# A two-block network with streamed weights: the first products of each FFN and MLP taken chunk by chunk, down products two steps behind

## What is computed

```python
def rms_norm(x, gain):
    y = xf * lax.rsqrt(jnp.mean(xf * xf, axis=-1, keepdims=True) + EPS)
    return (y * gain.astype(jnp.float32)).astype(x.dtype)

def swiglu(h, w13, w2):                       # hidden width 2816
    gate, up = jnp.split(h @ w13, 2, axis=-1)
    return (jax.nn.silu(gate) * up) @ w2

x = x + 0.5 * swiglu(rms_norm(x, ffn1_norm[l]), ffn1_w13[l], ffn1_w2[l])

def sq_relu_mlp(u, w1, w2):                   # hidden width 4096
    a = jnp.maximum(u @ w1, 0.0)
    return (a * a) @ w2

mod = (sc @ w_mod[l] + b_mod[l])[:, None, :]  # 1024 x 6144 for each of two l
mod_c = scc @ w_mod[l] + b_mod[l]             # the same weights for the context
```

## Time and profile before

| | us |
|---|---|
| three runs | 1719.1, 1723.56, 1721.61 |
| median | 1721.61 |
| profiled execution | 1721.9, of which the span 1720.1 |
| PE busy | 1617.6 (94%) |
| DVE busy | 1200.9 (70%) |
| ACT busy | 784.5 (46%) |

### The profile page before, as it was taken

One profiled execution on the slowest core, in us unless ns is written; L12 is line 12 of the kernel. 1 busy time (PEld: TensorE's weight loads), 2 busy tenths in 40 slices (PEclk: granted clock), 3 DMA queues, 4 the chain that ended last, 5 costly groups with the idle time before them and its releaser, 6 DMA issues.

```text
span 1720.1 us, 30317 instructions
## 1 busy us (share of the span) xinstructions
PE 1617.6 (94%) x12454; PEld 1545.4 (90%) x12454; DVE 1200.9 (70%) x1651; ACT 784.5 (46%) x1121; POOL 47.0 (3%) x46
## 2 busy tenths in 40 slices
PE   6999996999999899999789999999789999889999
PEld 6999996899999899999579999996358999879999
DVE  6887788888877677778647877654667656565654
ACT  5434458444445344446544444431445444454442
POOL 1000010100001100001001000000001000010000
PEclk9999998899999899999889999999799999989999
DMA  6766633476665366664124765621124554325450
GB/s 264 269 238 251 227 148 122 163 270 229 245 244 196 123 244 248 234 234 166 50 98 158 270 237 223 250 101 50 70 80 171 181 188 178 122 101 194 172 194 24
DMA packets 43434, 310.83 MB, mean 181 GB/s; under 512 B 4816, under 2 KB 5072, under 8 KB 6096
## 3 DMA queue, kind: packets, MB, share of 16 engines
q1 hardware_dynamic: 41904, 303.33, 47.5%
q0 software_dynamic: 864, 5.21, 0.9%
q10 hardware_dynamic: 576, 1.05, 0.2%
HBM read 308.52 MB, written 1.05 MB: 180 GB/s over the span
## 4 chain that ended last, share of the span: by engine, by line
PE 65%; DVE 11%; ACT 4%; issue 1%; POOL 1%; POOLq 0%; DVEq 0%; ACTq 0%
PE psum L1413 20%; PE psum L1418 19%; PE psum L1419 19%; DVE w_lo L806 4%; DVE buf L815 1%; PE psum L1574 1%; ACT w_hi L416 1%; PE psum L1472 1%; PE psum L1829 1%; DVE u_lo L906 1%; DVE x L885 1%; PE psum L1768 1%; POOL buf L372 1%; PE psum L1562 1%; DVE tiny L1319 0%
## 5 line engine op out<-in xcount | busy, mean ns | idle before, releaser
L1413 PE MATMUL psum<-u_hi,w_hi 128*128 128x256 f32 (+2 forms) x2608 | 761.1, 292 | 38.4 <-DVE u_lo L893 14.3
L1418 PE MATMUL psum<-u_lo,w_hi 128*128 128x256 f32 (+2 forms) x2608 | 750.3, 288 | 0.0
L1419 PE MATMUL psum<-u_hi,w_lo 128*128 128x256 f32 (+2 forms) x2608 | 750.0, 288 | 0.0
L806 DVE TENSOR_TENSOR w_lo<-raw,w_hi 128x1024 fp32r<-128x1024 f32 x480 | 565.3, 1223 | 163.0 <-ACT w_hi L416 162.8
L1413 PEld LDWEIGHTS psum<-u_hi,w_hi 128*128 128x128 f32 x2608 | 508.8, 195 | 48.5 <-issue 16.0
L416 ACT ACTIVATE w_hi<-raw 128x1024 fp32r<-128x1024 f32 x480 | 478.3, 1046 | 129.3 <-PE psum L1413 122.3
L1418 PEld LDWEIGHTS psum<-u_lo,w_hi 128*128 128x128 f32 x2608 | 509.2, 195 | 2.0
L1419 PEld LDWEIGHTS psum<-u_hi,w_lo 128*128 128x128 f32 x2608 | 508.5, 195 | 1.2
L1413 PE MATMUL psum<-hid_hi,w_hi 128*128 128x256 f32 x1220 | 346.4, 284 | 7.0 <-DVE hid_lo L1296 3.7
L1418 PE MATMUL psum<-hid_lo,w_hi 128*128 128x256 f32 x1220 | 345.4, 283 | 0.0
L1419 PE MATMUL psum<-hid_hi,w_lo 128*128 128x256 f32 x1220 | 345.3, 283 | 0.0
(11 more groups left out here) (205 smaller groups left out, 1007.9 us busy)
## 6 DMA issues: line engine op xcount, KB each, us to landing
raw<-stream SPq DMA_DIRECT2D x288, 1024.0 KB, 4.8
buf<-tab POOLq DMA_DIRECT2D x2, 768.0 KB, 4.6
x<-x_in SPq DMA_DIRECT2D x1, 1024.0 KB, 6.9
buf<-ctx_in POOLq DMA_DIRECT2D x1, 1024.0 KB, 5.1
buf<-poolmat POOLq DMA_DIRECT2D x1, 1024.0 KB, 5.1
out<-x ACTq DMA_DIRECT2D x4, 256.0 KB, 2.4
cst<-consts POOLq DMA_DIRECT2D x1, 864.0 KB, 9.0
buf<-late POOLq DMA_DIRECT2D x1, 640.0 KB, 4.3
```

The source lines that it names most:

```text
L806: ve.tensor_tensor(w_lo[:, u], raw[:, u], w_hi[:, u].bitcast(F32), ALU.subtract).then_inc(S.lo_ready, 1)
L1413: ins = te.matmul(dst, w_hi[:, w], hi, start=first, stop=False, skip_group_check=True)
L1418: te.matmul(dst, w_hi[:, w], lo, start=False, stop=False, skip_group_check=True)
L1419: return te.matmul(dst, w_lo[:, w], hi, start=False, stop=last, skip_group_check=True)
```

## The change

`by_chunk` takes several `up` units at once: for each k it waits for the operand, then makes the product of that k for every unit. In ffn1 to ffn3 these are the four units of steps 0 and 1, in ffn0 the two of step 0, in the MLPs the first three (the fourth follows by itself). The norm's product comes after them (in ffn0 after up 1) and goes to bank 0; step 2 of a SwiGLU uses bank 7. In a SwiGLU `down` j now follows up j+2, with four slots of 256 columns for `hid`, and the stream's order follows (`LAG`). `MODS_AT` moves modulation units: two each in steps 3 to 7, one from step 8. After hidden(j) DVE and ACT pump up to the unit before down j, so down j-1, up j+2 and the modulation units of j+2. Ahead of `rms` two more units of the FFN are split (up to its unit 7). The MLPs keep their lag of one. Left out below: the views `ff_hi`, `ff_lo`, `ff_hif`, the same `pump_to` and `early` edits in ffn2 and ffn3, and the bank of the ctx norm on DVE.

```diff
...
-MODS_AT = [0, 0] + [2, 1] * 4 + [1] * (FFS - 10)
+LAG = 2
+MODS_AT = [0, 0, 0, 2, 2, 2, 2, 2, 1, 1] + [1] * (FFS - 10)
...
-    FF_ORDER += [("up", _j)] * 2 + [("mod", _j)] * MODS_AT[_j] + [("down", _j - 1)] * (_j > 0)
-FF_ORDER += [("down", FFS - 1)]
+    FF_ORDER += [("up", _j)] * 2 + [("mod", _j)] * MODS_AT[_j] + [("down", _j - LAG)] * (_j >= LAG)
+FF_ORDER += [("down", FFS - _j) for _j in range(LAG, 0, -1)]
...
-NORM_BANK = {"ffn3": 0}
+NORM_BANK = {n: 0 for n in ("start", "wout", "ctx", "wo", "ffn3", "woe", "pool")}
...
+UP_BANK = [4, 5, 7] + [4 + _j % 2 for _j in range(3, FFS)]
...
-                    sc.activation(hid_hi[:, j % 2, 0:T], h32[:, 0:T], ACT.Copy).then_inc(S.hid_hi_ready, 1)
-
-                pump_to(c0 + ff_at("down", 0) - 1)
+                    sc.activation(ff_hi[:, j % 4, :], h32[:, 0:T], ACT.Copy).then_inc(S.hid_hi_ready, 1)
+
                 for j in range(FFS - 2):
                     hidden(j)
-                    pump_to(c0 + ff_at("down", j + 1) - 1)
+                    pump_to(c0 + ff_at("down", j) - 1)
...
-            pump_to(ff_at("down", 0) - 1)
+            pump_to(7)
...
-            gain_operand("ffn2_0", "wout", early=AT["ffn1"] + 4)
+            gain_operand("ffn2_0", "wout", early=AT["ffn1"] + 8)
...
-                    ve.tensor_tensor(t2.rearrange("p (k t) -> p k t", k=2), bank2(4 + par), over2(rstd[:, :]),
+                    ve.tensor_tensor(t2.rearrange("p (k t) -> p k t", k=2), bank2(UP_BANK[j]), over2(rstd[:, :]),
                                      ALU.mult).then_inc(S.up_scaled, 1)
...
-                    ve.tensor_tensor(hid_lo[:, par, 0:T], h32[:, 0:T], hid_hif[:, par, 0:T], ALU.subtract)\
+                    ve.tensor_tensor(ff_lo[:, j % 4, :], h32[:, 0:T], ff_hif[:, j % 4, :], ALU.subtract)\
                       .then_inc(S.hid_ready, 1)
 
-                pump_to(c0 + ff_at("down", 0) - 1)
                 for j in range(FFS - 2):
                     hidden(j)
-                    pump_to(c0 + ff_at("down", j + 1) - 1)
+                    pump_to(c0 + ff_at("down", j) - 1)
                     if j in MOD_READ:
                         read_modulation(MODG * int(name[3]) + MOD_READ.index(j))
                 hidden(FFS - 2)
+                pump_to(c0 + FFU - 1)
                 read_modulation(MODG * int(name[3]) + MODG - 1)
                 pump_to(c0 + FFU + 3)
                 hidden(FFS - 1)
...
             update_and_operand("wout", "ffn1", "ffn2_0", 1.0)
-            pump_to(AT["ffn1"] + 3)
...
-                te.matmul(psum[:, 7, 0:T], ones, buf[4][:, 0:T], start=True, stop=True).then_inc(S.ms_psum, 1)
-
-            def product(dst, c, at, hi, lo, first, last):
+                if name == "ctx":
+
+                    pe.wait_ge(S.v_out, 1)
+                te.matmul(psum[:, NORM_BANK.get(name, 7), 0:T], ones, buf[4][:, 0:T], start=True, stop=True)\
+                  .then_inc(S.ms_psum, 1)
+
+            def product(dst, c, at, hi, lo, first, last, begins=None):
 
                 w = slice((c % RING) * UNIT + at, (c % RING) * UNIT + at + P)
                 ins = te.matmul(dst, w_hi[:, w], hi, start=first, stop=False, skip_group_check=True)
-                if begun[0] != c:
+                if begun[0] != c if begins is None else begins:
 
                     ins.then_inc(S.unit_used, 1)
...
-            def all_k(c, i, dst, op=None, w=T):
+            def all_k(c, i, dst, w=T):
 
                 unit_ready(c, i)
                 for k in range(NC):
-                    if op:
-                        operand(op, k)
                     ins = product(dst, c, k * P, u_hi[:, k, 0:w], u_lo[:, k, 0:w], k == 0, k == NC - 1)
                 return ins
+
+            def by_chunk(c, op, dsts, w, shared):
+
+                n = len(dsts)
+                unit_ready(c + n - 1)
+                for k in range(NC):
+                    operand(op, k)
+                    for s in range(n):
+
+                        ins = product(dsts[s], c + s, k * P, u_hi[:, k, 0:w], u_lo[:, k, 0:w],
+                                      k == 0 and (s % 2 == 0 or not shared), k == NC - 1,
+                                      begins=k == (NC - 1 if s else 0))
+                        if k == NC - 1 and s % 2:
+                            ins.then_inc(S.up_ready, 1)
+                begun[0] = c + n - 1
...
-            def up(c, i, j, par, h0, op=None, between=lambda: None):
-
-                if not isinstance(j, int) or j >= 2:
+            def up(c, i, j, bank, h0):
+
+                if not isinstance(j, int) or j > 2:
 
                     pe.wait_ge(S.up_scaled, h0 + j - 1)
-                all_k(c, i, bank2(4 + par)[:, 0, :], op)
-                between()
-                all_k(c + 1, i, bank2(4 + par)[:, 1, :]).then_inc(S.up_ready, 1)
+                all_k(c, i, bank2(bank)[:, 0, :])
+                all_k(c + 1, i, bank2(bank)[:, 1, :]).then_inc(S.up_ready, 1)
 
             def swiglu(name, norm):
                 c0, h0, g0 = AT[name], STEPS[name], MODG * int(name[3])
 
-                def down(j, par, c, i=0, first=False, last=False):
+                def down(j, slot, c, i=0, first=False, last=False):
                     pe.wait_ge(S.hid_ready, h0 + j + 1)
-                    one_k(c, i, hid_hi[:, par, 0:T], hid_lo[:, par, 0:T], 0, first, last)
-
-                up(c0 + ff_at("up", 0), 0, 0, 0, h0, name, between=lambda: norm_sum(norm))
-
-                up(c0 + ff_at("up", 1), 0, 1, 1, h0)
-
-                pe.wait_ge(S.ms_ready, NRM[norm] + 1)
-                down(0, 0, c0 + ff_at("down", 0), first=True)
+                    one_k(c, i, ff_hi[:, slot, :], ff_lo[:, slot, :], 0, first, last)
+
+                first = [bank2(UP_BANK[j])[:, n, :] for j in range(2) for n in range(2)]
+                if name == "ffn0":
+                    by_chunk(c0, name, first[:2], T, True)
+                    up(c0 + 2, 0, 1, UP_BANK[1], h0)
+                else:
+                    by_chunk(c0, name, first, T, True)
+                norm_sum(norm)
                 for j in range(2, 10):
-                    up(c0 + ff_at("up", j), 0, j, j % 2, h0)
-                    down(j - 1, (j - 1) % 2, c0 + ff_at("down", j - 1))
+                    up(c0 + ff_at("up", j), 0, j, UP_BANK[j], h0)
+                    if j == 2:
+
+                        pe.wait_ge(S.ms_ready, NRM[norm] + 1)
+                    down(j - 2, (j - 2) % 4, c0 + ff_at("down", j - 2), first=j == 2)
                     if j in (4, 6, 8):
                         sum_modulation(g0 + j // 2 - 2, j // 2 - 2, last_unit(g0 + j // 2 - 2))
                 with pe.Fori(0, (FFS - 10) // 4) as i:
                     for s in range(4):
                         j, c = 10 + 4 * i + s, c0 + ff_at("up", 10 + s)
-                        up(c, 2 * i, j, s % 2, h0)
-                        down(j - 1, 1 - s % 2, c + 3, 2 * i)
+                        up(c, 2 * i, j, 4 + s % 2, h0)
+                        down(j - 2, s, c + 3, 2 * i)
                         if s == 2:
                             sum_modulation(g0 + 3 + i, 3, c0 + ff_at("mod", 13), 2 * i)
+                down(FFS - 2, (FFS - 2) % 4, c0 + FFU - 2)
                 if g0 < 2 * MODG:
                     sum_context(g0 // MODG)
-                down(FFS - 1, 1, c0 + FFU - 1, last=True)
+                down(FFS - 1, (FFS - 1) % 4, c0 + FFU - 1, last=True)
 
...
-                def up_pair(c, i, j, par, op=None, between=lambda: None):
-
-                    if not isinstance(j, int) or j >= 2:
-
-                        pe.wait_ge(S.up_scaled, h0 + j - 1)
-                    all_k(c, i, psum[:, 4 + 2 * par, 0:TS], op, TS)
-                    between()
+                def up_pair(c, i, j, par):
+
+                    pe.wait_ge(S.up_scaled, h0 + j - 1)
+                    all_k(c, i, psum[:, 4 + 2 * par, 0:TS], w=TS)
                     all_k(c + 1, i, psum[:, 5 + 2 * par, 0:TS], w=TS).then_inc(S.up_ready, 1)
...
-                up_pair(c0, 0, 0, 0, name, between=lambda: norm_sum(norm))
+                by_chunk(c0, name, [psum[:, 4 + n, 0:TS] for n in range(3)], TS, False)
+                norm_sum(norm)
+                all_k(c0 + 3, 0, psum[:, 7, 0:TS], w=TS).then_inc(S.up_ready, 1)
 
                 pe.wait_ge(S.ms_ready, NRM[norm] + 1)
-                up_pair(c0 + 2, 0, 1, 1)
                 down(0, 0, c0 + 4, first=True)
...
```

More of the change, by code:

```diff
@@ L279, in build @@
         hid_hif = hid_hi_t[:, :].bitcast(F32).rearrange("p (s t) -> p s t", s=2)
+        ff_hi = hid_hi_t[:, :].rearrange("p (s t) -> p s t", s=4)
+        ff_lo = hid_lo_t[:, :].rearrange("p (s t) -> p s t", s=4)
+        ff_hif = hid_hi_t[:, :].bitcast(F32).rearrange("p (s t) -> p s t", s=4)
         mod = mod_t[:, :].rearrange("p (l j c) -> p l j c", l=2, c=2)
@@ L630, in _ @@
                 square(NRM["ctx"], buf[3], b)
-            pump_to(AT["ffn2"] + 3)
+            pump_to(AT["ffn2"] + 7)
             act.wait_ge(S.ms_ready, NRM["ctx"] + 1)
@@ L675, in _ @@
```

(14 more changed lines are left out.)

## The result

| | before | after |
|---|---|---|
| median of 11 runs each, same chip | 1721.6 (1718.0 to 1724.7) | 1726.7 (1723.9 to 1727.4) |
| profiled execution | 1721.9, span 1720.1 | 1725.4, span 1723.5 |
| ratio after / before | | 1.0026, interval 1.0015 to 1.0036 |

The changed kernel takes 5.1 us more: a small loss that the interval separates from no change. What taking the units chunk by chunk brings at the starts is partly kept in ffn2 and ffn3 and more than spent again in ffn0, ffn1 and the MLPs.

What follows compares the result with a forecast made beforehand. PE was taken as the bound, with DVE second and slower in blocks with two modulation units. Phase terms, gains in ffn2 and ffn3 against losses in ffn0, ffn1 and the MLPs, summed to +3.9: 1721.6 to 1725.5 us, range 1717 to 1731.

Steps and rivals of the forecast that it cites:

- Part 1: Starts of ffn3 and ffn2: chunks remove 6.95 and 7.3 us lost, new waits come; net -2.6 and -3.0 us.
- part 4: Half clock after PE's waits: +2.1 us per MLP, +0.4 each in ffn2 and ffn3, +0.9 in ffn1.
- Part 2: FFNs, lag of two and new `MODS_AT`: split keeps 4.4 us slack; DVE-pinned ffn1 and ffn0 keep nothing, ffn1 +2.2 us.
- ffn0: the term that was mis-sized: ffn0: chunks at half clock, block 0 at 32.0 to 33.3 instead of 25.9; +2.7 to +4.0 us, 2.9 taken.
- a sign of being right: Among the signs named for a right forecast: ffn0 and ffn1 longer by 2 to 4 us.
- Part 3: MLP starts: PE waits about 5.5 us for `hid`; `down 0` moves by -1.4 us in mlp0, -0.1 in mlp1.
- DVE keeps up: Rival: gain at the starts stays, only the first `hid` is waited for; -16 us, 1705.5; chance 0.06.
- The clock: Rival: clock falls after waits of 1.3 to 2.2 us at SwiGLU starts; about +9 us, 1730.5; chance 0.36.
- The change of bank: Rival: `by_chunk` runs at half clock because its bank changes; about +30 us, 1755; chance 0.02.

Runs made afterwards that it cites:

- norm inside: Changed kernel with only the norm's product moved inside the chunks (in ffn0 between chunks and up 1): 1712.8 us, ratio 0.9944 to the kernel before.
- norm inside, waits filled: Changed kernel with the norm's product moved inside the chunks and 30 extra matmuls ahead of `down 0` in each MLP: 1710.2 us, ratio 0.9936 to before.
- the lag alone: Changed kernel with every FFN and MLP start taken back; lag of two, slots, `MODS_AT` and pumps stay: 1723.3 us, ratio 1.0009 to before.

## Why the prediction came out right

The forecast was 1725.5 in a range of 1717 to 1731; measured 1726.7. The signs of all six phases and the main mechanisms were right; that the total came so close is in part luck, since misses of up to 1.5 us, named below, partly cancel. The sum was +3.9; the profiled executions differ by 3.5 (spans 3.4), the medians by 5.1, and the 1.6 between these is the distance of two executions from their medians (0.3 above for before, 1.3 below for after).

- **Part 1, ffn3 and ffn2.** Forecast -2.2 and -2.6, measured -2.3 and -2.7: each of these phases is shorter, so both gains are real. DVE's blocks ran as forecast, to 1 us over the first eight (the prediction adds 7.9 and 1.45 to 9.1; that is 9.35, and blocks with two units took 9.3 to 9.6). The waits behind the start: first `hid` 1.3 forecast, about 1.25 later by the distance of starts (0.98 of it idle in the row); down 1 2.2 against 2.35 and 2.37. But the waits for down 2 and 4 (0.7 and 0.4 forecast) are missing, and in their place PE ran behind down 1 at a lower clock (part 4). The last `hid` isn't waited for at all, where 0.4 was left. So the sum is right by smaller misses that cancel.
- **Part 2, ffn1.** +3.1 against +3.5: wait for down 1 2.34, sum of group 2 1.72 (2.1 forecast), down 6 about 0.3 (0.6 forecast), and 1.67 at 393.77 for the split of down 5, which the prediction did not name for ffn1; the last block of the heavy units ends at 443.5 where it ended at 442.4 before, and PE has one `down` less done at that point, as the step had it. But PE doesn't wait for group 3 there, as it did before: its sum starts 1.2 us after DVE's last product, since the clock was low behind the wait for group 2.
- **ffn0: the term that was mis-sized.** +2.9 was taken, +1.4 measured, outside the 2 to 4 that were named as a sign of being right. I let the clock be at half until 19.7 and put block 0 at 32.0 to 33.3. It started at 31.37: the clock was up again from about 13 us on (the window below has 74 matmuls in 12 us, with PE idle 2.5 of it), and up 1 was done at 26.6 rather than 27 to 28.5. The rest is the clock again: before, it fell after the pair of waits (0.72 from 99.5 to 104.5); after, behind a wait of 1.7 for the sum of group 2, it did not, nor behind the wait of 2.35 for down 1 (third window). I had written that ffn0 pays the clock in both kernels. This part is chance: in the kernel after with the MLPs' waits filled, whose ffn0 is the same, the clock did fall behind both waits (the last two windows), and ffn0 took 213.5 us instead of 212.6, +2.3 against before. So of the 1.5 us between forecast and trace 0.9 is chance, and 0.6 is DVE's earlier start.

```profile
14.00:26.00 12.00, 9.50 (x74) 8.78 (x73) 10.57 (x9) 7.14 (x10) 5.27 (x5) 1.00 0.94 375
99.50:104.50 5.00, 5.00 (x43) 5.00 (x44) 3.51 (x6) 3.69 (x5) 0.00 (x0) 1.00 0.37 123
...
44.00:49.00 5.00, 3.80 (x32) 3.83 (x33) 4.86 (x6) 1.70 (x2) 0.00 (x0) 1.00 0.52 182
...
44.00:49.00 5.00, 4.00 (x21) 4.03 (x22) 4.86 (x6) 1.49 (x2) 0.00 (x0) 0.66 0.58 197
99.50:104.50 5.00, 5.00 (x31) 5.00 (x31) 3.68 (x5) 3.54 (x5) 0.00 (x0) 0.66 0.36 125
```

- **Part 3, the MLPs.** +0.7 and +2.0, measured +0.8 and +2.7. `down 0` began at 1319.18 and 1543.30 (forecast 1318.9 and 1542.5); in mlp1 the whole phase began 0.7 later, and within it `down 0` came as forecast (17.3 us behind the first product, 17.4 before). The waits were 5.4 from start to start (5.5 forecast). The miss in mlp1 lies behind the wait: 2.7 us where 2.1 was taken, since the half clock lasted 5.7 us there and 4.5 in mlp0.
- **Part 4, the clock.** It was taken as +2.1 for each MLP; the filling gave back 2.2 and 2.7. For the waits of 2.2 us in dense work no row had a price, and I took 0.4 net in ffn2 and ffn3 and 0.9 in ffn1. The clock did fall behind the wait for down 1 (the first three windows below: ffn1, ffn2, ffn3), and in ffn1 once more behind the sum of group 2 (the fourth). What that costs can be read where the same code ran with and without the fall. In the kernel with the old MLP start, ffn3 had the same wait of 2.37 and kept 1.00 (fifth window); PE then waited 0.66 and 0.50 for the splits of down 2 and 4, and the phase took 201.1 us, exactly as with the fall. So the fall costs nothing there (0.4 was taken): DVE sets the pace, and the slow matmuls only take the place of waits. In ffn1, "norm inside" kept 1.00 behind the wait of 1.7 for group 2 and took 204.7; "norm inside, waits filled" fell to 0.66 behind the same wait and took 205.7 (last two windows): 1.0, where 0.9 was taken.

```profile
353.00:358.50 5.50, 4.53 (x25) 4.56 (x26) 5.33 (x7) 1.46 (x2) 0.00 (x0) 0.69 0.58 219
...
620.00:625.00 5.00, 4.37 (x24) 4.40 (x25) 4.86 (x6) 1.12 (x2) 0.00 (x0) 0.66 0.66 236
937.00:942.00 5.00, 4.31 (x23) 4.34 (x24) 4.86 (x6) 1.18 (x2) 0.00 (x0) 0.66 0.64 228
409.00:413.00 4.00, 4.00 (x23) 4.00 (x22) 3.00 (x5) 3.26 (x4) 0.00 (x0) 0.57 0.15 61
...
936.50:942.00 5.50, 5.31 (x44) 5.34 (x45) 5.33 (x8) 0.68 (x1) 0.00 (x0) 1.00 0.74 279
...
403.80:409.00 5.20, 5.19 (x44) 5.20 (x45) 3.71 (x6) 3.68 (x5) 0.00 (x0) 1.00 0.39 156
403.00:408.00 5.00, 5.00 (x31) 5.00 (x31) 3.51 (x6) 3.67 (x5) 0.00 (x0) 0.66 0.34 139
```

- **The rivals.** "DVE keeps up" (-16): nearly that difference, -12.1, appears once DVE has less to do; with its real load it does not. "The clock" (+9): in this execution it fell where this rival said, in every FFN but ffn0, but mostly ahead of a wait for DVE that took it in. The change of bank: in the FFNs 96 matmuls in 11.4 us at 1.00, with another half bank every third and another bank every sixth; in the MLPs, whose chunks go to another bank every third matmul, the same 0.12 us and 1.00 (mlp0 below). The section "A second HAM failure mode: psum-queue depth-cycling" of the Trainium skill ("TensorE: Matmul & The Clock Gate") has a kernel whose clock went up and down as it cycled its banks, and puts that down to PE's short idle moments between the groups; this stretch has none (8.20 us busy of 8.20), and the clock stays up, so it neither shows nor denies the page's case.

```profile
1302.00:1310.20 8.20, 8.20 (x69) 8.20 (x69) 8.20 (x13) 7.07 (x12) 5.33 (x5) 1.00 0.19 56
```

- **What I did not weigh.** I wrote that the norm's product comes 3.3 us later, and priced that as one delay; nothing in the prediction asked what the same change would give with that product left early. That is where the study's largest effect, 14.3 us, lay. Nor is it settled why the lag alone cost 2 us less than its forecast. The trace puts it in ffn0: there group 3's last modulation product ends 121.9 us behind the phase's first matmul, 125.1 before; in ffn1 119.8 and 120.1. That would fit the four more splits that `pump_to(7)` puts ahead of ffn0's norm, but no run takes them back.

## What to carry to other kernels

When products are reordered to fill a thin phase, look for the product that starts a chain on another engine (here the norm's sum) and leave it where its input is ready: at the end of the filled phase it delays everything that the other engine supplies. Before a consumer is given more slack, check which of its inputs gets it; a lag between up and down helps `hid`, and does nothing for a weight split that still belongs to the next step. And compare the supplier's time for one block with the consumer's step: where it is longer for many steps, time gained at the start is given back before the phase ends, unless the supplier starts earlier by the same amount.
